# HGRN chunk states on TensorE: four products over 32 partitions in place of one over 128 with masked values

## What is computed

```python
def hgrn2_scan(seq, const, state):
    q, k, v, lf = seq
    cs = HGRN_CHUNK                                   # 32
    qc, kc, vc, lfc = (chunk(a, cs) for a in seq)
    a_cum = jnp.cumsum(lfc, axis=3)
    a_end = a_cum[:, :, :, -1]
    s_loc = jnp.einsum('bhcsk,bhcsv->bhckv', kc * jnp.exp(a_end[:, :, :, None] - a_cum), vc)

    def step(s_st, inp):
        a_j, sl_j = inp
        return jnp.exp(a_j)[..., None] * s_st + sl_j, s_st
    ...
    inter = jnp.einsum('bhctk,bhckv->bhctv', qc * jnp.exp(a_cum), s_in)
    ...
    out = inter + jnp.einsum('bhcts,bhcsv->bhctv', sc, vc)
```

## Time and profile before

| | us |
|---|---|
| median of 3 runs | 2463.77 (2463.47 to 2467.29) |
| the profiled execution, its own time | 2451.74 |
| its span | 2449.9 |
| forward block of the stage, first PE instruction to last copy | 537.23 to 578.89 |
| backward block | 605.09 to 645.03 |

### The profile page before, as it was taken

One profiled execution on the slowest core, in us unless ns is written; L12 is line 12 of the kernel. 1 busy time (PEld: TensorE's weight loads), 2 busy tenths in 40 slices (PEclk: granted clock), 3 DMA queues, 4 the chain that ended last, 5 costly groups with the idle time before them and its releaser, 6 DMA issues. The chain is left out here.

```text
span 2449.9 us, 31472 instructions
## 1 busy us (share of the span) xinstructions
PE 1977.4 (81%) x10528; PEld 1017.6 (42%) x10529; DVE 854.2 (35%) x1752; ACT 236.7 (10%) x517; POOL 680.4 (28%) x967
## 2 busy tenths in 40 slices
PE   3795759935788899899999976959778988787795
PEld 0342523323446454455555433324455544344442
DVE  0004720057545333233333344554343322222224
ACT  1102110122002000000000011001110000000001
POOL 0000000021101566456666400000005654444440
PEclk8895679977897999999999987979879999999998
DMA  9400047300206699999899575121238999999944
GB/s 378 181 1 1 0 176 291 121 1 1 91 0 279 229 410 411 414 408 393 348 409 393 218 309 216 69 107 65 90 130 358 415 420 422 422 422 420 419 194 189
DMA packets 99974, 601.65 MB, mean 246 GB/s; under 512 B 23200, under 2 KB 23435, under 8 KB 40444
## 3 DMA queue, kind: packets, MB, share of 16 engines
q1 hardware_dynamic: 66012, 516.78, 51.5%
q0 software_dynamic: 33888, 83.86, 9.2%
HBM read 590.50 MB, written 51.92 MB: 262 GB/s over the span
## 5 line engine op out<-in xcount | busy, mean ns | idle before, releaser
L1609 PE MATMUL bank<-moe_w,blk_xT 128*64 128x256 f32 x5632 | 679.4, 396 | 2.7 <-DVE blk_xT L1685 2.7
L1609 PEld LDWEIGHTS bank<-moe_w,blk_xT 128*64 128x64 f32 x5632 | 404.4, 142 | 220.1 <-issue 32.2
L1620 PE MATMUL bank<-moe_w,xt 128*64 128x512 f32 x1408 | 332.1, 592 | 1.5 <-DVE xt L1697 1.5
L1536 POOL DMA_INDIRECT ada_rows<-v_tokens,blk_gidx x264 | 272.5, 1032 | 140.2 <-issue 135.1
L451 PE MATMUL bank<-w_in_ring,xt 128*128 128x512 f32 x544 | 241.7, 604 | 13.0 <-DMA w_in_ring<-in_odd_w_in 10.2
L1685 DVE STREAM_TRANSPOSE blk_xT<-ada_rows 128x512 f32<-128x512 f32 x132 | 94.0, 712 | 450.8 <-PE bank L1609 427.1
L1552 POOL DMA_INDIRECT y_rows<-xt,blk_sidx x176 | 179.9, 1022 | 94.6 <-issue 48.4
L1704 DVE COPY xt<-bank 128x512 f32<-128x512 f32 x176 | 121.8, 692 | 149.3 <-PE bank L1620 149.3
L451 PEld LDWEIGHTS bank<-w_in_ring,xt 128*128 128x128 f32 x544 | 104.3, 194 | 148.1 <-issue 137.5
L1620 PEld LDWEIGHTS bank<-moe_w,xt 128*64 128x64 f32 x1408 | 100.9, 137 | 127.5 <-issue 100.5
L1668 ACT ACTIVATE xt<-bank 128x128 f32<-128x128 f32 x174 | 48.3, 278 | 1046.7 <-PE bank L1609 1046.7
(11 more groups left out here) (386 smaller groups left out, 1746.4 us busy)
## 6 DMA issues: line engine op xcount, KB each, us to landing
moe_w<-in_experts SPq DMA_DIRECT2D x128, 3072.0 KB, 31.0
ada_ring<-in_ada_w SPq DMA_DIRECT2D x12, 2048.0 KB, 17.2
w_out<-in_ada_w POOLq DMA_DIRECT2D x12, 2048.0 KB, 8.8
moe_w<-y_rows SPq DMA_DIRECT2D x24, 1024.0 KB, 20.5
w_in_ring<-in_even_w_in SPq DMA_DIRECT2D x8, 2048.0 KB, 12.6
w_in_ring<-in_odd_w_in SPq DMA_DIRECT2D x7, 2048.0 KB, 19.2
ada_rows<-v_tokens,blk_gidx POOLq DMA_INDIRECT x264
w_out<-in_even_w_out SPq DMA_DIRECT2D x1, 4096.0 KB, 12.3
```

Source lines behind the costliest of these rows:

```text
L1536: pool.indirect_dma_start(came[q][:, u], None, v_quarters, bass.IndirectOffsetOnAxis(ap=gidx[q][:, u:u + 1], axis=0), bounds_check=4 * n_t ...
L1609: last = nc.tensor.matmul(g.bank[1][64 * h:64 * h + 64, 0:HID], xT[:, k], w[:, s, (2 * k + h) * HID:(2 * k + h + 1) * HID], start=k == 0, ...
L1620: last = nc.tensor.matmul(g.bank[3][64 * h:64 * h + 64, :], hT[:, 64 * m:64 * m + 64], w[:, s, at:at + 512], start=m == 0, stop=m == 1)
```

## The change

`locate` now issues 16 products a tile. For head h and chunk c it takes the 32 partitions `own` of both `k1t` and the values themselves, and writes 128 columns of bank 2 + c: a bank holds a chunk now, with the heads side by side, where it held a head with the chunks side by side. Each product counts up `located`. POOL's part, `vmask` and the semaphore for it are gone. DVE's first step of a tile waits for all 16 products, and the steps read the new places. ACT's guard on `k1t` counts 16 a tile in place of 4.

```diff
--- before.py
+++ after.py
@@ -794,7 +794,6 @@
         E, D1, Q1, K1 = (work[:, i * HEADS * T:(i + 1) * HEADS * T] for i in range(4))
         reset = sb("reset", [P, T])
         dend = sb("dend", [P, HEADS * NCH])
-        vmask = sb("vmask", [P, 2, HEADS, TILE_CH * P])
         k1t = sb("k1t", [P, 2, HEADS, P])
         sc = sb("sc", [P, 2, 2, HEADS, P])
         st = sb("state", [P, HEADS, TILE_CH + 1, P])
@@ -916,8 +915,8 @@
                         act.wait_ge(prep, marks["K1", half.start])
                         nc.scalar.activation(K1[:, half], K1[:, half], ACT.Exp).then_inc(act_prep, 1)
 
-            (vmasked, turned, k1_ready, scored, masked, located, stated, out_ready, added) = (new_sem(g, x) for x in (
-                "v_masked", "k1_turned", "k1_ready", "hgrn_scored", "hgrn_masked", "s_loc_ready", "state_ready",
+            (turned, k1_ready, scored, masked, located, stated, out_ready, added) = (new_sem(g, x) for x in (
+                "k1_turned", "k1_ready", "hgrn_scored", "hgrn_masked", "s_loc_ready", "state_ready",
                 "hgrn_out_ready", "hgrn_added"))
             keep = g.tri_chunk[d]
             state_zeroed = new_sem(g, "state_zeroed")
@@ -943,12 +942,15 @@
 
                     def locate(n):
 
+                        i = tiles[n]
                         pe.wait_ge(k1_ready, n + 1)
-                        pe.wait_ge(vmasked, n + 1)
                         if n >= 1:
                             pe.wait_ge(stated, HEADS * TILE_CH * n)
                         for h in range(HEADS):
-                            nc.tensor.matmul(g.bank[2 + h][:], k1t[:, n % 2, h], vmask[:, n % 2, h], start=True, stop=True).then_inc(located, 1)
+                            for c in range(TILE_CH):
+                                own = slice(c * CHUNK, (c + 1) * CHUNK)
+                                nc.tensor.matmul(g.bank[2 + c][:, h * P:(h + 1) * P], k1t[own, n % 2, h], s["v"][own, i, h * P:(h + 1) * P],
+                                                 start=True, stop=True).then_inc(located, 1)
 
                     turn_keys(0)
                     locate(0)
@@ -976,19 +978,8 @@
                     for n, i in enumerate(tiles):
                         act.wait_ge(turned, n + 1)
                         if n >= 2:
-                            act.wait_ge(located, HEADS * (n - 1))
+                            act.wait_ge(located, HEADS * TILE_CH * (n - 1))
                         nc.scalar.activation(k1t[:, n % 2], g.bank[0][:].rearrange("p (h t) -> p h t", h=HEADS), ACT.Copy).then_inc(k1_ready, 1)
-
-                @block.gpsimd
-                def _(pool):
-                    for n, i in enumerate(tiles):
-                        if n >= 2:
-                            pool.wait_ge(located, HEADS * (n - 1))
-                        for h in range(HEADS):
-                            src = s["v"][:, i, h * P:(h + 1) * P].unsqueeze(1).broadcast_to([P, TILE_CH, P])
-                            last = pool.tensor_tensor(vmask[:, n % 2, h].rearrange("p (c v) -> p c v", v=P), src,
-                                                      g.chunk_of.unsqueeze(2).broadcast_to([P, TILE_CH, P]), ALU.mult)
-                        last.then_inc(vmasked, 1)
 
                 @block.vector
                 def _(dve):
@@ -1013,13 +1004,13 @@
                             gc = n * TILE_CH + m
                             for h in range(HEADS):
                                 if m == 0:
-                                    dve.wait_ge(located, n * HEADS + h + 1)
+                                    dve.wait_ge(located, (n + 1) * HEADS * TILE_CH)
                                 if gc >= 1:
 
                                     dve.wait_ge(stated, HEADS * (gc - 1) + h + 1)
                                 at = h * NCH + i * TILE_CH + c
                                 nc.vector.scalar_tensor_tensor(state(h, gc + 1), state(h, gc), dend[:, at:at + 1],
-                                                               g.bank[2 + h][:, c * P:(c + 1) * P], ALU.mult, ALU.add).then_inc(stated, 1)
+                                                               g.bank[2 + c][:, h * P:(h + 1) * P], ALU.mult, ALU.add).then_inc(stated, 1)
                         if n:
                             add(n - 1)
                     add(len(tiles) - 1)
```

## The result

The changed kernel takes **2437.36 us** (median of four runs, 2430.18 to 2445.92) against 2464.89 us for the kernel before, run beside it on the same chip: a ratio of 0.9897, 95% interval 0.9874 to 0.9920. That is 25.4 us less, with the interval 20 to 31. Of the executions reported further down, one of the changed kernel (3077.12 us) and one of a variant (6890.32 us) stand far above all others and are not in the ratios.

What follows compares the result with a forecast made beforehand. The prediction took PE work in the stage's two barrier-closed blocks as the bound: 7.3 (periods) + 12.3 (starts) - 2.0 (clock) = 17.6 us, so 2463.8 - 17.6 = 2446.2 us, range 2440 to 2457.

Steps and rivals of the forecast that it cites:

- starts: Each block up to its first output product, forecast at 12.0 us: gain 7.0 forward and 5.3 backward, 12.3 us.
- four periods: Steady tile periods, two a direction: from 7.87 to 6.05 us, a gain of 1.82 each, 7.3 us for four.
- the clock's loss: PE idling before `locate(1)` lets the clock fall, slowing output 0: 1.0 us lost each direction, 2.0 us in all.
- ends: End of a direction, two outputs of 2.99 us and one copy: unchanged, with at most 0.1 us of waiting.
- What bounds the kernel: The stage's two blocks, 41.66 and 39.94 us, each followed by a barrier: a microsecond gained there is gained in the program.
- the L970 strips: The output's M = 32 products, which ran side by side; taken as nearest in kind to size `locate` at 1.67 us.
- its 1.24: Alternative `locate` time: serial 3.8 us by the skill's reported 3.07 gain; about half a microsecond less in all.
- the serial rival: The row groups queue: `locate` 3.8 us, a period 8.2, total 2463.6 us, no change; chance 0.09.
- The serial rivals: Row groups queue, with loads hidden (2463.6 us, chance 0.09) or open at 0.21 us a pass (2485 us, chance 0.04).
- anything below 1.5 us for `locate` brings nothing more: In the steady period, DVE's own work of 5.9 us becomes the bound, just below the forecast 6.05.
- The nearly even pair, chain and queue: The steady period is `locate` + 4.39 us through DVE and `locate` + 4.37 through PE, both 6.05 at 1.67.
- the 12.0 us: Median of the runs before stood this far above the profiled execution; carried over unexplained, making the base 2463.8 us.

Runs made afterwards that it cites:

- again: The changed kernel without an edit, run once more beside the kernel before: ratio 0.9901 [0.9877, 0.9925], blocks 28.82 and 28.73 us.
- delayed: The changed kernel plus eleven idle DVE instructions (25.7 us stretch) between the stage and what follows: ratio to the kernel before 1.0023 [1.0008, 1.0037].
- chunk_outer: The changed kernel with the two loops of the 16 products exchanged, so four successive products use one row group and bank: ratio to the kernel before 1.0045.
- split_locate: The changed kernel with grouped outputs, ACT copying forward outputs, and `locate` split into three chunks, then the fourth: 2417.41 us, ratio to the kernel before 0.9863.
- act_copy: The changed kernel with the forward outputs copied by ACT instead of DVE: ratio to the kernel before 0.9942 [0.9925, 0.9959].
- grouped2: The changed kernel with each output's four full-width products first, then the sixteen M = 32 ones: ratio to the kernel before 0.9890 [0.9868, 0.9911].
- masks_kept: The changed kernel with POOL's masks, read by nothing, and PE's wait on them put back: ratio to the kernel before 0.9943 [0.9920, 0.9966].
- masks_early: The kernel before, with POOL's masks of a direction's first two tiles made one block earlier: ratio to the kernel before 1.0029 [1.0011, 1.0047].
- again2: The changed kernel without an edit, in a third comparison: 2425.11 us, ratio to the kernel before 0.9910 [0.9889, 0.9932].
- grouped_out: The changed kernel with each output's four full-width products first, then the sixteen M = 32 ones, in another comparison: ratio to the kernel before 0.9913.

## Why the prediction was right or wrong

The terms, in microseconds of gain, against the changed kernel's first profile. An end is what is left of a block after its start and two periods.

| term | forecast | measured |
|---|---|---|
| starts | 12.3 | 9.05 + 7.08 = 16.1 |
| four periods, less the clock's loss | 7.3 - 2.0 = 5.3 | 1.41 + 4.38 = 5.8 |
| ends | about 0 | -0.2 |
| the two blocks | 17.6 | 21.7 (24.1 in `again`) |

The time came out 8.8 us under the forecast of 2446.2. The blocks account for 4.1 of them, nearly all of it in the starts; the other 4.7 lie outside the blocks, and no experiment ties them to the change.

**What bounds the kernel: right.** A microsecond less in a block is one less in the program, as nearly as `delayed` can tell. So was the forecast that POOL's masks would leave no other wait behind.

**`locate`: right mechanism, sized too long.** The prediction took 1.67 us, from the L970 strips with a change of shape for each head. The trace has 1.11, below even the 1.3 that I gave as the least. A change of shape for each head isn't there to be paid, since `locate` stays with K = 32 in all its 32 passes; I had put four changes in a place that has one at each end. The estimate from the Trainium skill, "TensorE: Matmul & The Clock Gate", Part 3, was nearer: it reports 3.07 times for four K = 32 tiles, which made 1.24. Against the 3.50 of the 512-column products 1.11 is 3.15 times less, against the same products one group at a time (2.75, `chunk_outer`) it is 2.48 times less. The prediction let its 1.24 shorten the periods alone, though the four `locate`s of the starts go by it too. What the same page of the Trainium skill says in its LDWEIGHTS section, that a load of 32 rows takes as long as one of 128, also agrees, with a median of 187 ns for the loads of L952 against 189 for those of L965, but these loads don't queue: 32 of them would be 6 us (and not the 3.8 of the serial rival, to which I put them), and `locate` is 1.11. The serial rivals fall with that; `chunk_outer` shows what they would have looked like.

**The period: right at its bound, wrong on where it lay.** Forecast 6.05, measured 5.68. The statement that anything below 1.5 us for `locate` brings nothing more was wrong: DVE's own limit of 5.9 was summed from recorded lengths and gaps that overlap in part, and with the same work DVE went round in 5.68 and, in `split_locate`, 5.52. The nearly even pair, chain and queue, was right. At 1.11 the chain is `locate` + 4.57 (4.39 forecast), and PE's queue `locate` + 3.09 + 1.48 (4.37 forecast). Both gave back 0.2 us of the 0.56 by which `locate` was shorter. `act_copy` showed the one (DVE isn't it) and `grouped2` the other (PE's queue alone isn't it either).

**The starts: the step that failed.** I had the first output 12.0 us after the first transpose; it came at 9.94 and 10.19. That is 3.8 of the 4.1 us by which the blocks gained more than forecast. The chain from `locate(0)` to `locate(1)` took 4.60 for 4.39, so the error lies in the two `locate`s. "`locate(0)` at that clock ... 2.7" took 1.51 and 1.77 us, and `locate(1)`, put at 1.6 to 2.6, took 1.10. A little over half of this is the size again: even wholly at half clock `locate` takes 2.03 (531.51 to 533.54 in `masks_kept`). The rest is the clock, which the forecast held at 1.2 GHz through the whole of `locate(0)` and, by taking the middle of 1.6 and 2.6, through half of `locate(1)`. It rose within `locate(0)`, the turn of tile 1 behind it ran at full clock, and so did `locate(1)`, in both directions. In the serial rival I had the rise 8.4 us into the block, read from the kernel before, whose first 8.4 us hold an idle gap of 1.83 us. In the changed kernel, without that gap, the granted clock is 0.50 in the first 3.16 us of the block and 0.91 in the 2.60 after that.

```profile
535.84:539.00 3.16, 3.16 (x20) 2.94 (x24) 0.74 (x3) 0.60 (x1) 0.00 (x0) 0.50 0.01 3
539.00:541.60 2.60, 2.60 (x44) 2.32 (x40) 1.94 (x9) 0.60 (x1) 0.00 (x0) 0.91 0.00 0
```

`masks_kept` shows that in this kernel the early rise hangs on the wait: put back, it moves the rise to some 8 us, near the forecast's picture (first output at 12.91 and 11.94 us), and costs 8.4 to 10.7 us for 3.2 of waiting. The prediction counted the masks as a wait of that bare length and nothing more. That no gap is enough for an early rise can't be said: `masks_early` has none and the clock rose at 6.1 and 3.3 us, `chunk_outer` has none before 10.6 us and it stayed at 0.50 for 25.

**The clock's loss: right in kind.** PE idles 3.04 us before `locate(1)`, and output 0 of the forward direction ran at half clock in five of the seven profiles in which the start of that block is the changed kernel's (the first, `delayed`, `again2`, `grouped_out` and `grouped2`; not in `again` and `act_copy`), and in no backward direction of them. In those five blocks the clock had risen 3.4 to 3.7 us after the first transpose, in the nine others 4.1 to 4.9; why it falls in the one case and not in the other is not shown. Four periods at 5.68 would have gained 8.8; 3.0 of it were lost against 2.0 forecast, all in the forward direction and not half in each.

**From the blocks to the time: a term too sure.** I carried over the 12.0 us between the profiled execution of before and its median, and widened by 3.8 us, the spread of its three runs. The expert stages have two lengths, some 15 to 17 us apart together, in both kernels, and the median of the kernel before lay between 2446.5 and 2464.9 from one comparison to another. Had the sum been 21.7, the same steps would have given 2442.1, inside the range. The ratio's own gain, 25.4 [20, 31], has the stage's 21.7 to 24.1 in its interval and the forecast's 17.6 not.

**Not settled.** What sets the length of the expert stages. In the first of them the DMA share is 0.93 when it is long and 0.95 when it is short, which is the same DMA work over a longer time (0.95 of 576.85 and 0.93 of 590.32 us are 548 and 549), so the share names no cause, and no experiment here varied it. Nor is it settled what decides the clock at the starts and in `chunk_outer`.

## What to carry to other kernels

Small products with K = 32 belong side by side in the program's order, one after another in different row groups: the same 16 products cost 1.11 us in that order and 2.75 in the other at the same clock, and 5.03 where the clock was lost as well. A wait at the start of a block is to be priced with the clock that it holds back, here more than double its length. And a measured gain is best placed by the stretches that the change touches, with the spans' difference read only after the longest untouched stages have been held against each other.

## What was not expected of the hardware

- Busy records don't secure the clock. In `chunk_outer` PE was busy for 10.30 of 10.30 us in the backward direction with a granted clock of 0.67; in the changed kernel's period 5.68 of 5.68 gave 1.00. That products of one 32-row group follow one another in the former is not the whole of it: the same products in the forward direction had 1.00 over 7.32 of 7.32 us.
- POOL's TENSOR_TENSOR (f32, all operands in SBUF) doubled DVE's TENSOR_SCALAR beside it, 0.70 to 1.41 us for 128x1024, two of 128x512 from 1.13 to 2.48. DVE's state steps, which read a bank, were not slowed by the same masks in the kernel before: thirteen took 3.45 us, beside the masks of tile 2 (547.47 to 551.51), and twelve take 3.18 with no POOL work beside them in the changed kernel, 0.265 each in both. The Trainium skill, "SBUF — State Buffer", "Who interferes with whom", has GpSimd and some of DVE's modes exclude each other at a shared pair of ports for a whole instruction. That one form is hit and the other not fits it; the records show a longer instruction and can't tell waiting from running slowly.
- A change between M = 128 and M = 32 products costs about 0.17 us at full clock (0.99 us for six of them).
